# One-core kernel of two transformer blocks with a mixture of experts: stage ends reordered, routing rewritten, further blocks behind one branch, last rows loaded earlier

## The reference

```python
h = _modulate(_rmsnorm(x, norm1_g), shift1, scale1)
z = h @ w_in
y = concat([_gmlp_mixer(...), _rwkv7_mixer(...)]) @ w_out
x = x + gate1 * y
h = _modulate(_rmsnorm(x, norm2_g), shift2, scale2)
x = x + gate2 * _hier_moe(h, ...)         # top 2 of 32 experts
return _rmsnorm(x, final_norm_g)
```

## Time and profile before

| | |
|---|---|
| median of three executions | 3078.43 us (3071.15 to 3080.0) |
| profiled execution, its own time | 3087.37 us |
| its span, first to last instruction | 3085.6 us |
| mean granted TensorE clock | 0.970 |
| PE busy | 2895.9 us (94%) |
| DVE, ACT, POOL busy | 58%, 35%, 15% |
| L721, 128x512 matmuls | 384 in 167.6 us |
| HBM traffic | 146 GB/s over the span, 389 GB/s in the expert loop |

### The profile page before, as it was taken

How to read it: one execution, slowest core, us unless ns; L and a number is a source line. 1 busy time by engine, 2 the same in 40 slices (tenths; PEclk the granted TensorE clock), 3 DMA queues, 4 the chain that set the end, 5 groups by cost and what they waited for, 6 DMA issues and landing times. The chain is left out here.

```text
span 3085.6 us, 47695 instructions
## 1 busy us (share of the span) xinstructions
PE 2895.9 (94%) x19486; PEld 2179.9 (71%) x19486; DVE 1779.8 (58%) x2743; ACT 1094.2 (35%) x1700; POOL 454.5 (15%) x352
## 2 busy tenths in 40 slices
PE   8999999999999999989999999998898999999991
PEld 6877644676777777767747768687688777777760
DVE  3332222485566666555434626253874899999984
ACT  2111100122455454452231313222531566665652
POOL 2222100021322222213131101010000000000001
PEclk9999999999999999999999999998898999999995
DMA  4111031663222112121221211016346899999975
GB/s 167 45 38 45 15 129 55 184 194 123 61 61 63 55 55 62 56 100 51 68 56 34 65 29 60 7 59 202 129 166 224 329 396 397 398 398 398 397 286 231
DMA packets 290940, 454.44 MB, mean 147 GB/s; under 512 B 15760, under 2 KB 157584, under 8 KB 290752
## 3 DMA queue, kind: packets, MB, share of 16 engines
q1 hardware_dynamic: 283696, 426.06, 39.6%
q0 software_dynamic: 7056, 25.69, 2.1%
HBM read 389.77 MB, written 61.93 MB: 146 GB/s over the span
## 5 line engine op out<-in xcount | busy, mean ns | idle before, releaser
L1016 PE MATMUL psum<-x_hi,w_hi 128*128 128x512 f32 x512 | 210.6, 411 | 2.3 <-PEq L100 1.6
L1207 DVE TENSOR_TENSOR fox_pT_lo<-psum,fox_pT_hi 128x512 fp32r<-128x512 f32 (+2 forms) x192 | 107.1, 558 | 180.7 <-ACT fox_pT_hi L1146 171.6
L1018 PE MATMUL psum<-x_hi,w_lo 128*128 128x512 f32 x512 | 201.0, 393 | 0.0
L1017 PE MATMUL psum<-x_lo,w_hi 128*128 128x512 f32 x512 | 199.9, 390 | 0.0
L3065 ACT CAST hi_d<-land_d 128x2048 fp32r<-128x2048 f32 x66 | 122.8, 1909 | 141.0 <-PE psum L2935 141.0
L721 PE MATMUL psum<-wo,yT 128*128 128x512 f32 x384 | 167.6, 593 | 2.9 <-PEq L100 1.5
L1704 PE MATMUL psum<-hT,wr 128*128 128x512 f32 x384 | 167.1, 593 | 0.0
L3120 DVE TENSOR_TENSOR lo_d<-land_d,hi_d 128x2048 fp32r<-128x2048 f32 x66 | 148.3, 2289 | 21.5 <-ACT hi_d L3065 21.5
L3120 DVE TENSOR_TENSOR lo_g<-land_g,hi_g 128x2048 fp32r<-128x2048 f32 x66 | 150.6, 2283 | 0.1
L1157 ACT ACTIVATE fox_p<-fox_p,fox_bias 128x256 f32<-128x256 f32 (+7 forms) x128 | 99.6, 778 | 118.5 <-DVE fox_bias L1193 114.9
L180 PE MATMUL psum<-x_lo,w_hi 128*128 128x512 f32 x352 | 138.3, 393 | 0.0
(11 more groups left out here) (526 smaller groups left out, 7049.2 us busy)
## 6 DMA issues: line engine op xcount, KB each, us to landing
land_g<-in_moe_w_gate SPq DMA_DIRECT2D x66, 1024.0 KB, 7.9
land_u<-in_moe_w_up SPq DMA_DIRECT2D x66, 1024.0 KB, 8.9
land_d<-in_moe_w_down SPq DMA_DIRECT2D x66, 1024.0 KB, 9.4
ada<-in_ada_w SPq DMA_DIRECT2D x24, 1024.0 KB, 5.6
y_slots<-yb SPq DMA_DIRECT2D x33, 512.0 KB, 10.3
w<-in_w_in SPq DMA_DIRECT2D x27, 512.0 KB, 3.9
w_land<-in_w_kv_shared SPq DMA_DIRECT2D x23, 512.0 KB, 4.1
w_land<-in_w_in SPq DMA_DIRECT2D x23, 512.0 KB, 3.9
```

The lines of the kernel that those rows point to most:

```text
L1016: nc.tensor.matmul(bank[:], hi[:, d, :], E.x_hi[:, d, cols], start=(d == 0), stop=False)
L1017: nc.tensor.matmul(bank[:], hi[:, d, :], E.x_lo[:, d, cols], start=False, stop=False)
L1018: last = nc.tensor.matmul(bank[:], lo[:, d, :], E.x_hi[:, d, cols], start=False, stop=(d == ND - 1))
```

## The change

It has ten parts.

- The two loads of `E.w0` move from `stage_constants` to SP of `stage_memory_kv`.
- `stage_out` takes the last token tile half by half instead of chunk by chunk.
- `keep_warm` of 6 (last step but one) and 12 (last step) ahead of `turn` in FoX, and of 6 for the last head of the memory attention.
- RWKV: the evacuation of MT and N becomes `states(c)`; for the first three pairs it stands in the next pair's front, after the product of `bt` by `e2`; the `keep_warm` of 10 goes.
- End of mixing: router of tile 6 and a `keep_warm` of 9 stand ahead of the last transposes, DVE evacuates half of these, the final `keep_warm` goes from 18 to 4 and the one of 8 goes. The zeros are written in six parts in steps 2 to 7.
- Routing: rank matmuls in the one-pass type (fp32r) with `before` and ones made by POOL and ACT, ranks by one scan over (expert, tile), `nover` by one comparison and one reduction, one joint place for each (token, expert) that includes the overflow, expert offset from the numbers of group and expert, tables in fp32r, `at_part` in halves after `at_block`, `idx` before the splits of the weights.
- SP waits for block 0's gather before it loads weights of block 1; block 0's rows are modulated and split in halves, the second by ACT; the table of further experts (`ovcmp` and after) is computed later; `keep_busy` counts are adapted.
- One branch (`filled > 1`) stands round the loop of further blocks on every engine, with the waits inside it, and the number is read before the last result; inside it the loop has no branch.
- `cx` and the gain get their SBUF at the place of the second buffers ("odd"), and SP loads them in the step of the last block, after the store of the result of block 31.
- Combine: no weighting on ACT; DVE does two multiply-and-add instructions per tile, each waiting for one gather.

```diff
-                win = A["w_in"][0].rearrange("(c p) n -> p c n", p=P)
...
+                    by_chunk = [(c, hf) for c in range(NY) for hf in range(2)]
+                    by_half = [(c, hf) for hf in range(2) for c in range(NY)]
+                    for c, hf in by_chunk if t < NT - 1 else by_half:
...
+                    if n >= STEPS - 2:
+                        keep_warm(nc, E, pe, ringP, 6 if n < STEPS - 1 else 12)
                     turn(n, 0)
...
+                    else:
+                        keep_warm(nc, E, pe, ringD, 6)
                     attn.turn(pe, h)
...
-                    if c + 1 < NPAIR:
-                        keep_warm(nc, E, pe, ringA, 10)
...
+                    if c >= 1:
+                        states(c - 1)
                     dve.wait_ge(S_["exp2"], c + 1)
...
+                    if t == NT + 3:
+                        router(t - 5)
+                        keep_warm(nc, E, pe, ringA, 9)
...
-                    if t == NT + 3:
-                        keep_warm(nc, E, pe, ringD, 8)
-                keep_warm(nc, E, pe, ringD, 18)
+                keep_warm(nc, E, pe, ringD, 4)
...
+                    if t < 2 + ZERO_PARTS:
+                        part = slice((t - 2) * ZEROS, (t - 1) * ZEROS)
...
-            with eng.Fori(0, OVER - 1) as j:
-                with eng.If(filled > j + 1):
+            with eng.If(filled > 1):
+                begin()
+                with eng.Fori(0, OVER - 1) as j:
                     step(j)
...
+                sp.wait_ge(xg_in[0], 16)
                 for x in ("g0", "g1", "u0"):
                     load(x, 1)
...
+                    if isinstance(b, int) and b + 1 == LOOPED:
+                        sp.wait_ge(M["up_full"], LOOPED - 1)
+                        for t in range(NT):
+                            sp.dma_start(E.cx[t][:], x_rows[t * P:(t + 1) * P, :]).then_inc(E.cx_landed[t], 16)
...
-                link(dve, V.memset(base[:, 0, :], 0.0))
-                for t in range(NT):
-                    link(dve, V.tensor_tensor(base[:, t + 1, :], base[:, t, :], rank_b[:, n32 + t * EXPERTS:n32 + (t + 1) * EXPERTS], ALU.add))
...
+                link(dve, V.tensor_copy(tile_sums, rank_b[:, n32:2 * n32].rearrange("p (t e) -> p e t", t=NT)))
+                link(dve, V.tensor_tensor_scan(flat_e(upto_tile[:]), keep, flat_e(tile_sums), 0.0, ALU.mult, ALU.add))
...
+                link(dve, V.tensor_tensor(passed, count, edges, ALU.is_gt))
+                link(dve, V.tensor_reduce(nover[:], passed, X, ALU.add))
...
-                    link(dve, V.tensor_tensor(pick[:], one32[:], over_t(over_at[:], EXPERTS), ALU.mult))
-                    link(dve, V.tensor_reduce(over[:], pick[:], X, ALU.add))
...
+                    link(dve, V.scalar_tensor_tensor(at[:], expert[:], float(P), at[:], ALU.mult, ALU.add))
                     link(dve, V.tensor_copy(E.slot[k][:], at[:]))
...
+                dve.wait_ge(R["table"], 1)
+                V.tensor_copy(idx[:], rank_b[:, 0:BLOCKS]).then_inc(R["idx"], 1)
                 lo("g0", 0)
                 lo("g1", 0)
...
+                        link(dve, V.scalar_tensor_tensor(x[t][:], y[0][t][:], E.weight[0][:, t:t + 1], x[t][:], ALU.mult, ALU.add))
+                        dve.wait_ge(y_in[1][t], 16)
+                        V.scalar_tensor_tensor(x[t][:], y[1][t][:], E.weight[1][:, t:t + 1], x[t][:], ALU.mult, ALU.add).then_inc(summed, 1)
```

More of the change, by code:

```diff
@@ L641, in turn, with evacuate @@
             last.then_inc(ring.full, 1)
-    def evacuate(self, act, t):
+    def evacuate(self, act, t, halves=(0, 1)):
         nc, ring = self.nc, self.ring
-        for h in range(2):
+        for h in halves:
             act.wait_ge(ring.full, ring.nth(("t", t, h)))
@@ L2568, in _ @@
                             act.wait_ge(ringD.full, ringD.nth(("r", t - 6)))
-                        norm.evacuate(act, t - 4)
+                        norm.evacuate(act, t - 4, halves=(0, 1) if t < NT + 3 else (0,))
                     if t + 1 < NT:
@@ L3052, in _ @@
                 nc.scalar.activation(gexp[:], gexp[:], ACT.Exp).then_inc(R["gexp"], 1)
+                nc.scalar.copy(ones_r, E.ones[:]).then_inc(R["masks"], 1)
+                act.wait_ge(R["consts"], 2)
+                nc.scalar.copy(before_r, before[:]).then_inc(R["masks"], 1)
                 act.wait_ge(R["ssub"], 1)
```

318 lines of the change are left out of this document (175 added, 143 removed).

## The result

The changed kernel takes 3024.24 us (median of four executions, 3022.78 to 3027.42) against 3079.22 of the kernel before in the same measurement: a ratio of 0.9825, 95% interval 0.9808 to 0.9843. The forecast was 3011 with a range of 2994 to 3035. The gain is 55.0 us; 67.0 were forecast.

The account below looks back on a forecast made before the run. PE was taken as busy nearly throughout, leaving gains only in its gaps, low-clock stretches and the two ends. Terms summed to 67.0 us; 3078.4 − 67.0 = 3011.4, given as 3011, range 2994 to 3035.

Parts of the forecast that it names:

- (a): Constants stage: without the two loads the barrier comes earlier; gain 2.9 us, bounds 0 and 4.4.
- (d): Out stage, last tile: taken by halves, one residual of 1.45 us is hidden in each of two layers; gain 2.9.
- (g): Routing up to the first expert matmul: shorter DVE work, earlier index, faster gather, overlapped halves; net gain 14.4 us, bounds 9 and 17.
- (i): Combine: rows loaded during the last block, first product earlier; length 41.3 against 52.6 us, gain 11.3, bounds 7 and 12.5.
- (h): Between last block and combine: one branch instead of 14 passes; gain 10.4 us, bounds 2 and 10.9.
- (b): Memory attention, last head: fillers in PE's idle hold the clock; gain 2.4 us, bounds 0 and 3.0.
- (c): End of FoX: fillers of 6 and 12 matmuls against idle and low clock; gain 2.5 us, bounds 0 and 3.4.
- (e): RWKV, three times: DVE evacuates the states earlier, so Q starts 2.5 us sooner; gain 7.4, bounds 0 and 8.
- (f): End of mixing: transposes and router at the high clock, fewer fillers; gain 13.3 us, low end 10, high 13.5.
- gathers are no faster alone: Rival, chance 0.10: gathering 128 rows may need 6 to 8 us regardless; routing loses 4.2, combine 4; 3019.6.
- the fixed stall: Rival, chance 0.15: the 11.9 us before combine are one far taken branch's stall, mostly kept; 8 less gain, 3019.
- the rival on the loop: Rival, chance 0.03: a 2.3 us gap per expert block drops the clock; 31 blocks cost 146, about 3157, slower.

Follow-up runs that it names:

- passes_old: Changed kernel with the one branch round the loop of further blocks replaced by 14 passes with a branch each, as before: 3032.15 us.
- rwkv_old: Changed kernel with the RWKV part alone undone (fillers of 10 back, evacuation of MT and N behind the next pair's front): 3036.11 us.
- cx_late: Changed kernel with residual rows and gain loaded at combine's start and the expert stage's second buffers at their former SBUF places: 3022.70 us.
- cx_placed: Changed kernel with second buffers at former SBUF places, residual rows still loaded early, into them and dead routing tables: 3016.82 us.

## Why the prediction was right, and where it was short

The direction, the order of the terms and the range held; the point was 13 too low. Of this, 5.7 is the step "I carry that over": the profiled execution of before lay 8.9 above the median then known, that of after 3.2 above its own. At 3087.4 it was slower than every other execution of before on record (3071.2 to 3084.8); where its 8.9 lay is not known, since no second trace of before exists. The other 7.1 is in the terms, and would be 9.0 without the 1.9 of layer 0, which no edit touches and which is luck. No run undid (a), (d), the new arithmetic of (g) or that of (i); these are read from the pair of traces. The high end of the range is not the sum it names: two rivals at 3028 and 13 more are 3041, and one rival with the 13 is 3033.

- (a), (h): right. (a) came out at 4.6, just above its upper bound of 4.4, since the clock did rise earlier. (h) was 10.2 of 10.4, and passes_old shows the cause, 14 passes at 0.7, though not for the reason that the forecast gave.
- (d): 2.9 as forecast, but as 0.75 in layer 0 and 2.2 in layer 1 where 1.45 each was priced. The sum is right in part by luck.
- (b), (c): the mechanism was right, the size is a draw: 2.7 and 2.2 at the last head and FoX's end in this pair of traces, 0.7 and 1.5 when undone. The other 2.7 of the memory stage lie elsewhere and no run undid them; the same code gives 185.5 to 188.2.
- (e): 7.2 by the rows, as forecast, 1.0 in the stage. The step that failed was to sum a stage of PE's work from engine waits alone: the forecast had no term for pauses without a releaser, though the trace of before shows them (0.75 within the same group). The 1.0 sets a short draw of the old code (575.3, against 580.7 in rwkv_old) against a long one of the new (574.3, of 568.6 to 574.5).
- (f): 12.1 of 13.3 at the end, since the clock fell once more at 1.46 of idle; 1.4 went in front of it, within the scatter of the steps with and without the early zeros (205.2 to 207.0 from the stage's start to the last rows, 205.6 before). The zeros cost nothing that can be seen.
- (g): the DVE parts were right to 0.2 (8.6 for both choices, 0.9 to the index). The gather came 2.1 later than priced: the step "2.6 and an issue of 1.3" took the issue from the row below, beside which DVE ran instructions of 0.7 at most, and the change puts a split of 2.3 there. That is a quarter of the 8.2 of the rival "gathers are no faster alone", with another cause. The 1.7 for block 0 was 1.45.
- The loop: "no instruction in it changes, so it keeps its period" failed, by 0.06 on average against before. The addresses changed; with the old places it is 18.40, 0.06 below before, and that difference no run explains.
- (i): 9.6 of 11.3. The first product came 4.5 behind the first issue, as forecast (4.4). Then POOL's issues beside DVE's products stretch to 1.6 and 1.9 (0.94 at first), and once DVE waits 1.18 for a gather; cx_late shows that the early rows are worth 7.2.

The issue in the trace of before:

```profile
2380.90 1.33 POOL L3035 DMA_INDIRECT xg<-n_rows,idx  x1 [32.11 <-DVE idx L3195]
```

Of the rivals, the fixed stall is refuted; the clock that doesn't hold occurred in one place of three, behind an idle of 1.46, so the 2.26 of the rival on the loop is no safe bound; the loop's lengthening did occur, at a thirtieth of the size that would have decided.

## What to carry to other kernels

Price a seam from its rows and it comes out; then ask what the moved work runs beside: a POOL-issued gather beside a long DVE instruction was a miss here. A stage of short matmuls can wait for its own instructions; where PE pauses and nobody is named, look at the packets of the instruction queue, and expect the pauses to move with every instruction added ahead. Passes of a loop that is never entered stand in the source view, with their times. A loop that repeats thirty times is worth a look at its period in hundredths of a microsecond after any change of buffer places. And when one trace is the basis, look for stretches with two levels before carrying its distance to the median over.

## What the runs showed of the hardware

- The place of the second buffers in SBUF moved PE's period with PE full and the same instructions: 18.40 (cx_late, cx_placed) against 18.43 and 18.60 in turn (after). e_x_hi1 lay at byte 51520 in the slow blocks, at 195168 in the fast ones; shifting it to 51552, with hi_g0 from 109152 to 109280, left 18.59. What it collides with, and which buffer, is open.
- PE paused 0.4 to 3.0 us with no releaser in the RWKV stage, each of 39 times until 1.24 to 1.72 after a 16 KB packet of the instruction queue q8. 19 of these pauses stood with the DMA engines idle; behind a burst of 2.5 MB of stores one was 1.3 or 3.0, and gone when the burst came later. After 3.0 the next group ran at the low clock.
- An indirect gather was issued in 0.94 to 1.15 us with DVE quiet. One that began while DVE ran a 128x2048 TENSOR_TENSOR took 2.9 to 3.1, or 1.69, and ended 0.8 to 1.0 after that instruction. One that began within 0.03 of such an instruction's start took 0.94 (before, 2382.54).
- A small POOL memset behind a gather held DVE until the gather was issued; a bare semaphore increment in its place did not, DVE began 0.2 before the issue.
- Fourteen loop passes round a branch that leads past the body cost 10 us more than one such branch: 0.7 a pass on DVE, with two packets of 8 KB on the instruction queue meanwhile.
